# A fixed first expert, turns of half the length and a gate on the expert rows, in a two-block transformer kernel

## Chip, cores and metric

One core of a Trainium2 chip runs the whole program. The metric is the device time of one execution in microseconds (us). Weights come from the chip's memory (HBM) through one queue of DMA transfers, which the SyncE program (SP) issues. TensorE (PE) multiplies, VectorE (DVE) and ScalarE (ACT) prepare operands and empty PSUM, and GpSimd (POOL) does little.

## What is computed

256 tokens of width 1024 go through a first block (branches of attention and gated recurrence, then 32 small experts) and a second block of two layers: attention and a dense feed-forward layer, then a state-space mixer and, last, a layer of 8 large experts. The change touches only this last layer and the final norm. All is in float32. Cut to what matters:

```
def moe_swiglu(h, w_router, w_gate, w_up, w_down):      # h: 256 tokens x 1024
    top_vals, top_idx = lax.top_k(t @ w_router, 2)      # 2 of 8 experts a token
    gates = softmax over the two, spread over 8 columns
    for e in range(8):                                  # w_gate, w_up: 1024 x 2816, w_down: 2816 x 1024
        out = out + gates[:, e:e + 1] * swiglu(t, w_gate[e], w_up[e], w_down[e])
...
    x = x + g2[:, None, :] * y                          # g2: the layer gate, 1024 numbers
return rmsnorm(x, final_norm)
```

The inputs are drawn by `setup_inputs(seed=0)`. Computed from the reference with these inputs, the router sends 33, 58, 115, 44, 96, 45, 47 and 74 tokens to experts 0 to 7.

## The kernel before

**Ranks.** After the router's logits, VectorE counts the tokens of each expert and sorts the experts by count (`order_dve`, line 2096). The experts of ranks 0 to 3 are the heavy ones. Each has 128 slots for tokens, and PE multiplies it in three float32r passes per product (`split_product`, line 262), for which ACT makes the high part of each weight tile (line 192) and DVE the low part (line 202). The experts of ranks 4 to 7 are the light ones. They are computed in two pairs, numbers 4 and 5 in `RANKS`; each expert of a pair has 64 slots (`SIDE`), the two share the array by halves, and the product is in plain float32 straight from the loaded tile (lines 2458 and 2513). An expert whose tokens don't fit its slots gets a block of its own at the end (`over_cases`), with its weights loaded once more.

**Units.** An expert's weights come in units of two rows of 128 by 1024 columns, 1 MiB each. The 2816 hidden columns are three chunks, 0 to 2, of 1024, 1024 and 768 columns. A chunk of a heavy expert is 4 units of the gate matrix and 4 of the up matrix (768 KiB each in chunk 2), and the down matrix is 11 units. A pair has twice as many. The ring holds 8 units. SP issues the load of unit u as soon as unit u-8 has been let go: for a heavy expert that is when DVE has made the low parts of the unit, which it may do up to four parts (two units) ahead of PE; for a pair it is when PE has multiplied the two units of a step. One semaphore per slot holds SP.

**The order by hand.** `PHASES` says in which order experts are read in ("in": gate and up) and out ("out": down). It runs heavy 0 (in, out), pair 4 (in), heavy 1 (in, out), pair 4 (out), heavy 2 (in, out), pair 5 (in), heavy 3 (in, out), pair 5 (out). I call a stretch of work on heavy experts between two of pairs a heavy turn, and the other way round a light turn. All five engines' programs follow this list. The first load of the layer waits for the sorted order (SP line 3957), because every expert's address comes out of it.

**Around a turn.** After the gate product of a chunk PE turns the chunk before it (`mid_pe`, line 2260), and scatters the rows of an expert that has ended into token order (`scatter_pe`, through line 252), which DVE adds to `total` (line 2372). Before that the down product, which lies in PSUM, is scaled by the slots' gates and split into a high part by ACT (line 2342) and a low part by DVE (line 2407). During a light turn ACT and DVE make up to four parts of the next heavy turn ahead.

**The end.** `last_dve` multiplies `total` by the layer gate `gate_b` (line 3924), adds it to `x` (line 3925), and then comes the final norm: squares on DVE and ACT (lines 853, 840), two small operations on POOL, and the scaled output (line 3930), which SP stores.

Of the kernel before, what the change touches and what calls it, by code (L numbers as in the profile page):

```python
# [301 lines left out]
def row_parts(n, kt=KD):  # L302
# [17 lines left out]
INS = [i for phase, i in PHASES if phase == "in"]  # L320
OUTS = [i for phase, i in PHASES if phase == "out"]

# [6 lines left out]
def heavy_after(phase, i):  # L329

    n = PHASES.index((phase, i)) + 1
    return next((k for ph, k in PHASES[n:] if ph == "in" and k < HEAVY), None)

# [35 lines left out]
def block(nc, A, out):  # L369
# [180 lines left out]
    def moe_tensors(M, rows_, where):  # L550
# [11 lines left out]
        if M.three:  # L562
# [3 lines left out]
            M.key, M.top, M.order = sb("key" + t, [P, n], where=where), sb("top" + t, [P, n], where=where), sb("order" + t, [P, n], U32, where=where)  # L566
            M.order_f, M.chosen = sb("order_f" + t, [P, n], where=where), sb("chosen" + t, [P, n, n], where=where)
# [112 lines left out]
    moe2.gain8, moe2.acc = None, total  # L680
# [126 lines left out]
    for phase, i in PHASES:  # L807
        sides = range(len(RANKS[i]))
        if phase == "in":
            for ch in range(len(moe2.chunks)):  # L810
                for g in range(2):
                    for k0 in range(0, KD, moe2.kper):
                        for side in sides:
                            ranked_in_unit(i, side, g, ch, k0)
# [4 lines left out]
        units_after[phase, i] = len(fine.units)  # L819
# [1215 lines left out]
    def gates_pool(g, M):  # L2035
        g.iota(M.iota[:, :], pattern=[[1, M.n_exp]], base=0, channel_multiplier=0,
               allow_small_or_imprecise_dtypes=True).then_inc(*consts.up())
        g.iota(M.slots[:, :], pattern=[[1, P]], base=0, channel_multiplier=0,
               allow_small_or_imprecise_dtypes=True).then_inc(*consts.up())
        g.iota(M.beyond[:, :, :], pattern=[[-SIDE if M.three else P, M.blocks], [1, P]], base=M.cap, channel_multiplier=0,  # L2040
               allow_small_or_imprecise_dtypes=True).then_inc(*consts.up("iota", M.name))
# [76 lines left out]
    def ranked_table_dve(v, st, M):  # L2118
# [4 lines left out]
        v.tensor_scalar(M.over[:, 0:HEAVY], top[:, 0:HEAVY], 8.0 * P, None, ALU.is_gt).then_inc(*d.up())  # L2123
# [191 lines left out]
    def expert_act(a, run, i):  # L2315
# [16 lines left out]
        a.wait_ge(*run.multiplied(last_down(run, i)))  # L2332
        if M.three:
            y_hi_act(a, run, i)
        else:
            a.copy(M.ysb[:, :], run.banks.of(st.name, "down", i)).then_inc(*st.act.up("y", i))
# [27 lines left out]
    def scatter_dve(v, run, i):  # L2364
        M, st = run.moe, run.st
        for t in range(NT):
# [3 lines left out]
            elif run is run2:  # L2370
                v.wait_ge(*st.pool.of("total"))
# [3 lines left out]
    def expert_dve(v, run, i, e, slots):  # L2375
# [14 lines left out]
        if M.three:  # L2390
            slot_gates_dve(v, run, i)
            y_lo_dve(v, run, i)
# [10 lines left out]

    def y_lo_dve(v, run, i):
# [4 lines left out]
        run.banks.empty(st.dve, st.name, "down", i)  # L2409

    IN_CHUNKS = [(i, ch) for i in INS for ch in range(len(moe2.chunks))]

    def chunk_before(i, ch):
        n = IN_CHUNKS.index((i, ch))
        return IN_CHUNKS[n - 1] if n else None

    def turned_in(i, ch):

        b = chunk_before(i, ch)
        return b if b and (ch or b[0] >= HEAVY) else None

    def phase_before(phase, i):
        n = PHASES.index((phase, i))
        return PHASES[n - 1] if n else (None, None)
# [36 lines left out]
    def in_pe(p, i):  # L2463
        st = S["moe2"]
        held = phase_before("in", i)
        for ch, n in enumerate(moe2.chunks):
            cuts = [slice(c, min(c + 512, n)) for c in range(0, n, 512)]
            for g in range(2):
                ps = banks.take(p, "moe2", ("gate", "up")[g], i, ch)
                if ch == 0 and g == 0:  # L2470
                    if i == 0:
                        constant_products(p, ps, ident, 16)
                    if held[0] == "out" and held[1] >= HEAVY:
                        banks.let_go("moe2", "down", held[1])
                (heavy_in_product_pe if i < HEAVY else light_in_product_pe)(p, i, g, ch, ps, cuts)
                if g == 0:
                    if ch == 0 and held[0] == "out":
                        scatter_pe(p, run2, held[1])
                    if turned_in(i, ch):
                        mid_pe(p, run2, *turned_in(i, ch))  # L2480
                if i == 0 and ch == 1:
                    light_step_pe(p, g)
# [42 lines left out]
    def ranked_pe(p):  # L2525
        for step in range(4):
            pair_step_pe(p, 0, step)
        for phase, i in PHASES:
            (in_pe if phase == "in" else out_pe)(p, i)
# [4 lines left out]
    def hi_after(a, i, u):  # L2534
        fine_split.make_hi(a, min(fine_split.end(u) + PARTS, fine_split.end(out_unit(i))))

    def lo_after(v, i, u):
        fine_split.make_lo(v, min(fine_split.end(u) + PARTS, fine_split.end(out_unit(i))))

    def parts_ahead(phase, i, n):  # L2540

        k = heavy_after(phase, i)
        return fine_split.first[run2.units[k, 0, 0, 0, 0]] + n if k is not None else 0
# [21 lines left out]
    def in_act(a, i):  # L2565
        M, st = moe2, S["moe2"]
        for ch, n in enumerate(M.chunks):
            if i < HEAVY:
                hi_after(a, i, in_unit(i, 0, ch))
            a.wait_ge(*run2.multiplied(in_unit(i, 0, ch)))  # L2570
            if chunk_before(i, ch):
                a.wait_ge(*st.dve.of("mid", *chunk_before(i, ch)))
            a.activation(M.sil_row[:, 0:n], banks.of("moe2", "gate", i, ch)[:, 0:n], ACT.Silu).then_inc(*st.act.up("sil", i, ch))  # L2573
            banks.empty(st.act, "moe2", "gate", i, ch)
            if turned_in(i, ch):
                turned_mid_act(a, *turned_in(i, ch))
            if i == 0 and ch == 1:
                light_step_act(a, 0)
            if i < HEAVY:
                hi_after(a, i, in_unit(i, 1, ch))  # L2580
            if i == 0 and ch == 1:
                light_step_act(a, 1)
        if i >= HEAVY:
# [1469 lines left out]
```

## Time and profile before

| what | value |
|---|---|
| three runs | 2307.22, 2312.49, 2314.65 us, median 2312.49 |
| the profiled execution | 2311.4 us; its span of instructions is 2309.5 us |
| busy share of the span | PE 85%, PEld 61%, DVE 47%, ACT 37%, POOL 2% |
| HBM read | 659.90 MB, 286 GB/s over the span |
| first load of the last layer issued | 1575.86 us |
| last down product multiplied | about 2289.2 us |

The span is the time from the first instruction to the last; the runs' times lie around it. Rows of the profile give times in us from the start of the span.

### The profile page before, as it was taken

What the parts mean: (1) busy time and instruction counts of PE and PEld (TensorE: products, weight loads), DVE (VectorE), ACT (ScalarE), POOL (GpSimd) and SP (SyncE); (2) the same over time, 40 slices, a digit from 0 to 9 for tenths busy, and PEclk for the clock granted to TensorE, in tenths of its full rate; (3) what the DMA queues carried; (4) which work ended last, traced back from release to release, by engine and by line L of the source; (5) the groups of instructions that cost most, each with busy time, mean ns of one, the idle gap of its engine ahead of it and who ended that gap; (6) DMA issues with size and microseconds to landing.
All of it is one profiled execution on the core that took longest, in us unless ns stands there. A gap on an engine that the chain in (4) does not pass through costs nothing.

```text
span 2309.5 us, 29186 instructions
## 1 busy us (share of the span) xinstructions
PE 1952.6 (85%) x12033; PEld 1401.9 (61%) x12033; DVE 1085.1 (47%) x1661; ACT 854.1 (37%) x1153; POOL 44.9 (2%) x110
## 2 busy tenths in 40 slices
PE   6989988996656556698999998998987999997996
PEld 6968767762111111357899797877843775843772
DVE  3945556431211110233555577767830873930772
ACT  4432344310000000234444357846710754720760
POOL 0010200000000000000000000000000000000000
PEclk9989998999898888899999999999999999999998
DMA  8463662489999999859445454407999999999996
GB/s 269 168 219 110 210 244 74 189 315 393 409 409 409 409 409 409 302 198 369 147 165 201 164 155 160 143 1 286 367 383 405 406 372 409 391 379 405 407 379 244
DMA packets 227523, 663.02 MB, mean 287 GB/s; under 512 B 20100, under 2 KB 28840, under 8 KB 227124
## 3 DMA queue, kind: packets, MB, share of 16 engines
q1 hardware_dynamic: 219628, 652.92, 74.0%
q10 hardware_dynamic: 7752, 8.11, 1.3%
q8 instruction: 99, 1.62, 0.3%
q14 instruction: 44, 0.36, 0.1%
HBM read 659.90 MB, written 1.10 MB: 286 GB/s over the span
## 4 chain that ended last, share of the span: by engine, by line
PE 52%; DMA 25%; DVE 12%; ACT 7%; issue 3%; POOL 0%; ACTq 0%; SPq 0%; DVEq 0%; POOLq 0%
PE psum L263 11%; PE psum L265 11%; PE psum L264 11%; PE psum L252 6%; DMA ring<-in_w_expert_down 6%; DMA ring<-in_w_expert_up 5%; DMA ring<-in_w_expert_gate 5%; DMA ring<-in_moe_w_gate 4%; PE psum L2458 3%; DMA ring<-in_moe_w_up 3%; PE psum L2513 2%; DVE w_lo L202 2%; PE psum L2738 2%; ACT w_hi L192 2%; PE psum L1175 1%
## 5 line engine op out<-in xcount | busy, mean ns | idle before, releaser
L202 DVE TENSOR_TENSOR w_lo<-ring,w_hi 128x1024 fp32r<-128x1024 f32 (+1 forms) x498 | 579.4, 1187 | 389.4 <-ACT w_hi L192 380.6
L192 ACT CAST w_hi<-ring 128x1024 fp32r<-128x1024 f32 (+1 forms) x498 | 502.9, 1021 | 335.8 <-PE psum L265 297.0
L2738 PE MATMUL psum<-ring,hT 128*32 128x512 f32 x960 | 145.5, 738 | 117.1 <-DMA ring<-in_w_expert_gate 63.8
L2458 PE MATMUL psum<-ring,xg_pair 128*64 128x512 f32 (+1 forms) x768 | 159.8, 561 | 38.8 <-DMA ring<-in_moe_w_gate 19.9
L2738 PEld LDWEIGHTS psum<-ring,hT 128*32 128x32 f32 x960 | 30.3, 124 | 228.0 <-issue 97.5
L263 PE MATMUL psum<-w_hi,xg_hi 128*128 128x512 f32 (+1 forms) x384 | 146.4, 381 | 7.3 <-DVE w_lo L202 7.3
L264 PE MATMUL psum<-w_hi,xg_lo 128*128 128x512 f32 (+1 forms) x384 | 145.1, 378 | 0.0
L265 PE MATMUL psum<-w_lo,xg_hi 128*128 128x512 f32 (+1 forms) x384 | 144.8, 377 | 0.0
L2458 PEld LDWEIGHTS psum<-ring,xg_pair 128*64 128x64 f32 x768 | 58.9, 137 | 136.7 <-issue 134.8
L2372 DVE TENSOR_TENSOR x<-x,psum 128x1024 f32<-128x1024 f32 x14 | 17.1, 1221 | 219.8 <-PE psum L252 219.8
L2760 PE MATMUL psum<-ring,midT 128*32 128x512 f32 x480 | 69.9, 712 | 44.0 <-DMA ring<-in_w_expert_down 43.5
L263 PE MATMUL psum<-h_f_hi,w_hi 128*128 128x256 f32 x352 | 100.6, 286 | 2.2 <-DVE h_f_lo L886 2.2
L264 PE MATMUL psum<-h_f_hi,w_lo 128*128 128x256 f32 x352 | 100.3, 285 | 0.0
L265 PE MATMUL psum<-h_f_lo,w_hi 128*128 128x256 f32 x352 | 100.2, 285 | 0.0
L263 PEld LDWEIGHTS psum<-w_hi,xg_hi 128*128 128x128 f32 x384 | 72.6, 189 | 24.4 <-issue 7.7
L2513 PE MATMUL psum<-ring,midT 128*64 128x512 f32 x352 | 78.4, 596 | 7.1 <-DMA ring<-in_moe_w_down 7.1
L265 PEld LDWEIGHTS psum<-w_lo,xg_hi 128*128 128x128 f32 x384 | 72.7, 189 | 14.3
L264 PEld LDWEIGHTS psum<-w_hi,xg_lo 128*128 128x128 f32 x384 | 72.7, 189 | 13.9
L2573 ACT ACTIVATE hT<-psum 128x1024 f32<-128x1024 f32 (+1 forms) x18 | 17.1, 951 | 166.8 <-PE psum L2458 166.8
L263 PE MATMUL psum<-w_hi,midT_hi 128*128 128x512 f32 x176 | 70.1, 398 | 3.0 <-DVE w_lo L202 3.0
L263 PE MATMUL psum<-h_mix_hi,w_hi 128*128 128x256 f32 x224 | 63.8, 285 | 7.8 <-DVE w_lo L202 7.8
L2760 PEld LDWEIGHTS psum<-ring,midT 128*32 128x32 f32 x480 | 14.2, 121 | 91.9 <-DMA ring<-in_w_expert_down 65.4
(697 smaller groups left out, 3799.0 us busy)
## 6 DMA issues: line engine op xcount, KB each, us to landing
ring<-in_moe_w_down SPq DMA_DIRECT2D x88, 1024.0 KB, 7.9
ring<-in_w_expert_gate SPq DMA_DIRECT2D x32, 2048.0 KB, 17.2
ring<-in_moe_w_gate SPq DMA_DIRECT2D x64, 1024.0 KB, 13.2
ring<-in_moe_w_up SPq DMA_DIRECT2D x64, 1024.0 KB, 14.5
ring<-in_w_expert_down SPq DMA_DIRECT2D x30, 2048.0 KB, 18.1
ring<-in_w_expert_up SPq DMA_DIRECT2D x28, 2048.0 KB, 17.9
ring<-in_ada_w SPq DMA_DIRECT2D x24, 2048.0 KB, 11.7
ring<-in_moe_w_gate SPq DMA_DIRECT2D x32, 768.0 KB, 12.1
```

The lines of the kernel that those rows point to most:

```text
L192: a.copy(self.buffers(n, src.shape)[0], src).then_inc(*self.hi_made.up())
L202: v.tensor_tensor(lo, src, hi.bitcast(F32), SUB).then_inc(*self.lo_made.up())
L252: ins = p.matmul(o, l, r, start=n == 0, stop=n == len(terms) - 1)
L263: p.matmul(o, l[0], r[0], start=start, stop=False)
L264: p.matmul(o, l[1], r[0], start=False, stop=False)
L265: return p.matmul(o, l[0], r[1], start=False, stop=stop)
L1175: ins = p.matmul(ps[32 * quarter:32 * quarter + 32, 0:256], cond[:, k:k + 1].to_broadcast([P, 32]), w[quarter // 2][:, k, c0:c0 + 256], st ...
L2372: v.tensor_tensor(M.acc[:, t, :], M.acc[:, t, :], run.banks.of(st.name, "scatter", i, t), ADD).then_inc(*st.dve.up("acc", i, t))
L2458: ins = p.matmul(ps[r, cut], moe2.xg_pair[:, i - HEAVY, k0 + k, r], w[side][:, k, cut], start=k0 + k == 0, stop=k0 + k == KD - 1)
L2513: ins = p.matmul(ps[r, cut], M.midT[:, k0 + k, r], w[side][:, k, cut], start=first, stop=last)
L2738: ins = p.matmul(ps[slots_of(j), g * 512:(g + 1) * 512], M.xg[:, 2 * q + k, slots_of(j)], w[:, j, k, :], start=2 * q + k == 0, stop=2 * q ...
L2760: ins = p.matmul(ps[slots_of(j), cut], M.midT[:, q, slots_of(j)], w[:, j, cut], start=q == 0, stop=q == 3)
```

## The change

It has three parts. First, expert 0 always takes rank 0: its key gets 4096 added, so that it comes first in the sort whatever its count, and SP loads its first eight units with a known address while the ring's last slots of the mixer become free, before the router has run. Second, the list is by chunk instead of by phase: a heavy turn is now two chunks, or the third chunk and the down product, and between them lies one chunk of a pair or its down product. Third, the layer gate is multiplied onto the expert's rows before they are split (`y_gated_dve`), the scattered rows are added straight into `x`, and `total`, its clearing on POOL and the two operations at the end go away. Besides, 12 small products on a constant stand before the last scatter, and the light experts' rows are gathered earlier (after chunk 0 and in chunk 1 of heavy 0).

```
+FIXED = 0
+FIRST_KEY = 4096.0
-PHASES = (("in", 0), ("out", 0), ("in", 4), ("in", 1), ("out", 1), ("out", 4),
-          ("in", 2), ("out", 2), ("in", 5), ("in", 3), ("out", 3), ("out", 5))
+OUT = 3
+STEPS = ((0, 0), (0, 1), (4, 0), (0, 2), (0, OUT), (4, 1), (1, 0), (1, 1), (4, 2), (1, 2), (1, OUT), (4, OUT),
+         (2, 0), (2, 1), (5, 0), (2, 2), (2, OUT), (5, 1), (3, 0), (3, 1), (5, 2), (3, 2), (3, OUT), (5, OUT))
...
-    moe2.gain8, moe2.acc = None, total
+    moe2.gain8, moe2.acc = None, x
+    y_gated = total[:, 0, :]
...
+            g.memset(M.less[:, FIXED:FIXED + 1], -FIRST_KEY).then_inc(*consts.up())
+            g.iota(M.less[:, FIXED + 1:], pattern=[[1, M.n_exp - FIXED - 1]], base=FIXED + 1, channel_multiplier=0,
...
-        settle(v, v.scalar_tensor_tensor(M.key[:, :], counts, 8.0, M.iota[:, :], MUL, SUB), d)
+        settle(v, v.scalar_tensor_tensor(M.key[:, :], counts, 8.0, M.less[:, :], MUL, SUB), d)
...
     def y_hi_act(a, run, i):
-        a.wait_ge(*st.dve.of("selgT", i))
-        a.activation(M.y_split[0], run.banks.of(st.name, "down", i), ACT.Copy, scale=M.slot_gate[:, 0:1]).then_inc(*st.act.up("y", i))
+        a.wait_ge(*st.dve.of("y_gated", i))
+        a.copy(M.y_split[0], y_gated).then_inc(*st.act.up("y", i))
...
+    def y_gated_dve(v, run, i, multiplied):
+        v.wait_ge(*multiplied)
+        v.wait_ge(*gates_loaded.of("layer", 1))
+        v.wait_ge(*st.dve.of("selgT", i))
+        v.scalar_tensor_tensor(y_gated, run.banks.of(st.name, "down", i), M.slot_gate[:, 0:1], gate_b[:, 1, :], MUL, MUL)...
...
     def y_lo_dve(v, run, i):
-        v.scalar_tensor_tensor(M.y_split[1], run.banks.of(st.name, "down", i), M.slot_gate[:, 0:1], M.y_split[0].bitcast(F32),
-                               MUL, SUB).then_inc(*st.dve.up("y_lo", i))
+        v.tensor_tensor(M.y_split[1], y_gated, M.y_split[0].bitcast(F32), SUB).then_inc(*st.dve.up("y_lo", i))
...
     def ranked_pe(p):
-        for phase, i in PHASES:
-            (in_pe if phase == "in" else out_pe)(p, i)
+        for i, ch in STEPS:
+            if ch == OUT:
+                out_pe(p, i)
+            else:
+                in_pe(p, i, ch)
+        constant_products(p, banks.held_by("moe2", "selgT", OUTS[-1])[:, 512:1024], ident, 12)
...
     def in_dve(v, i, ch):
...
+        if (i, ch) == (HEAVY, 0):
+            ranked_table_dve(v, st, M)
         if i >= HEAVY:
-            fine_split.make_lo(v, parts_ahead("in", i, PARTS))
+            fine_split.make_lo(v, parts_ahead(i, ch, PARTS))
...
-        g.memset(total[:, :, :], 0.0).then_inc(*S["moe2"].pool.up("total"))
...
-        settle(v, v.tensor_tensor(total[:, :, :], total[:, :, :], gate_b[:, 1, :].unsqueeze(1).to_broadcast([P, NT, D]), MUL), d)
-        settle(v, v.tensor_tensor(x[:, :, :], x[:, :, :], total[:, :, :], ADD), d, "x")
...
     def last_act(a):
-        a.wait_ge(*st.dve.of("x"))
+        a.wait_ge(*S["moe2"].dve.of("acc", OUTS[-1], 0))
...
     def sync(s):
+        experts = {0: FIXED}
         for u in range(len(ring.units) - SLOTS, len(ring.units)):
             if ring.emptied is not None:
                 s.wait_ge(*ring.emptied[u])
-        s.wait_ge(*S["moe2"].dve.of("order"))
-        experts = {}
+            if u % SLOTS == u - len(ring.units) + SLOTS:
+                fine.load(s, 2 * (u % SLOTS) + 2, experts)
+        ordered = False
+        for i, ch in STEPS:
+            if ch == 0:
+                if i and not ordered:
+                    s.wait_ge(*S["moe2"].dve.of("order"))
```

## Rows read from the trace of the kernel before

**Rows 1.** The page, part 2: the span in 40 equal slices of 57.7 us.

```profile
GB/s 269 168 219 110 210 244 74 189 315 393 409 409 409 409 409 409 302 198 369 147 165 201 164 155 160 143 1 286 367 383 405 406 372 409 391 379 405 407 379 244
```

**Rows 2.** The windows view of all engines: stretch, length, busy, clock, DMA share, GB/s.

```profile
1575.00:1587.00 12.00, 8.96 (x64) 8.89 (x64) 4.48 (x17) 6.39 (x11) 0.00 (x0) 0.86 0.82 321
1587.00:1697.00 110.00, 109.08 (x523) 85.03 (x524) 86.74 (x80) 76.07 (x80) 0.00 (x0) 1.00 0.98 372
...
1790.00:1897.00 107.00, 104.14 (x484) 82.10 (x482) 89.22 (x86) 75.86 (x78) 0.00 (x0) 0.98 0.98 387
...
1940.00:2047.00 107.00, 104.83 (x488) 81.73 (x489) 89.47 (x83) 73.60 (x76) 0.00 (x0) 1.00 0.99 383
2047.00:2143.00 96.00, 76.39 (x376) 29.97 (x372) 4.79 (x4) 5.41 (x6) 0.00 (x0) 1.00 1.03 407
2143.00:2248.00 105.00, 102.07 (x478) 80.71 (x480) 88.88 (x86) 75.22 (x78) 0.00 (x0) 1.00 1.00 391
...
2284.00:2310.00 26.00, 7.25 (x26) 3.72 (x24) 12.03 (x9) 2.26 (x3) 0.94 (x2) 0.71 0.11 44
```

**Rows 3.** The waits view of SP's queue, 1500 to 2310 us.

```profile
SPq L3957 <- DVE order L2101: 28.0, 1, 28.0
```

**Rows 4.** The chain that ended last, in order of time: start, us, what.

```profile
1587.10 0.43 PE psum L263
...
1621.24 0.87 PE psum L2260 x8
1622.11 1.88 PE psum L252 x16
...
1687.45 13.91 PE psum L2458 x64
...
1828.79 0.87 PE psum L2260 x8
...
1849.27 0.87 PE psum L2260 x8
...
1891.27 7.02 PE psum L2513 x32
...
2039.66 13.91 PE psum L2458 x64
...
2242.28 7.02 PE psum L2513 x32
```

**Rows 5.** The timeline of PE where heavy turns begin and the last unit lands.

```profile
1792.88 0.68 PE L263 MATMUL psum<-w_hi,xg_hi 128*128 128x512 f32 x1 [2.11 <-DVE w_lo L202]
...
1939.78 0.47 PE L263 MATMUL psum<-w_hi,xg_hi 128*128 128x512 f32 x1 [1.24 <-DVE w_lo L202]
...
1942.83 0.50 PE L263 MATMUL psum<-w_hi,xg_hi 128*128 128x512 f32 x1 [1.42 <-DVE w_lo L202]
...
2144.92 0.47 PE L263 MATMUL psum<-w_hi,xg_hi 128*128 128x512 f32 x1 [2.10 <-DVE w_lo L202]
...
2285.54 3.65 PE L2513 MATMUL psum<-ring,midT 128*64 128x512 f32 x16 [1.38 <-DMA ring<-in_moe_w_down]
```

**Rows 6.** The chain again: the end.

```profile
2289.23 1.12 ACT ysb_hi L2342
2290.38 1.29 DVE ysb_lo L2407
2291.81 3.45 PE psum L252 x8
...
2296.70 2.30 DVE total L3924
2299.03 2.30 DVE x L3925
```

**Rows 7.** The timeline of DVE in the first light turn: the overflow table's first and last operation.

```profile
1720.58 0.15 DVE L2123 TENSOR_SCALAR over<-top 1x4 f32<-1x4 f32 x1
...
1725.30 0.16 DVE L2133 CAST table<-tf 1x10 int32<-1x10 f32 x1
```

More of the change, by code:

```diff
@@ L326, in out_before, with heavy_after, heavy_end @@
     return OUTS[n - 1] if n else None
-def heavy_after(phase, i):
-    n = PHASES.index((phase, i)) + 1
-    return next((k for ph, k in PHASES[n:] if ph == "in" and k < HEAVY), None)
+def heavy_after(i, ch):
+    n = STEPS.index((i, ch)) + 1
+    return next((step for step in STEPS[n:] if step[0] < HEAVY), None)
+def heavy_end(i, ch):
+    n = STEPS.index((i, ch))
+    while n + 1 < len(STEPS) and STEPS[n + 1][0] < HEAVY:
+        n += 1
+    return STEPS[n]
 class Moe:
@@ L806, in block @@
     units_after = {}
-    for phase, i in PHASES:
+    for i, ch in STEPS:
         sides = range(len(RANKS[i]))
[L809 to L814, printed above, removed]
+        if ch != OUT:
+            for g in range(2):
+                for k0 in range(0, KD, moe2.kper):
+                    for side in sides:
+                        ranked_in_unit(i, side, g, ch, k0)
         else:
@@ L818, in block @@
                     ranked_out_unit(i, side, k0)
-        units_after[phase, i] = len(fine.units)
+        units_after[i, ch] = len(fine.units)
+    assert len(ring.units) % SLOTS == 0, len(ring.units)
     split_ends = (split.end(unit["out", 1]), len(split.parts))
@@ L2391, in expert_dve @@
             slot_gates_dve(v, run, i)
+            y_gated_dve(v, run, i, run.multiplied(last_down(run, i)))
             y_lo_dve(v, run, i)
@@ L2461, in light_in_product_pe, with in_pe @@
                 fine.empty(st.pe, u)
[L2463 to L2482, printed above, removed]
+    def in_pe(p, i, ch):
+        n = moe2.chunks[ch]
+        ended = out_ended(i, ch)
+        cuts = [slice(c, min(c + 512, n)) for c in range(0, n, 512)]
+        for g in range(2):
+            ps = banks.take(p, "moe2", ("gate", "up")[g], i, ch)
+            if g == 0:
+                if (i, ch) == (0, 0):
+                    constant_products(p, ps, ident, 16)
+                if ended is not None and ended >= HEAVY:
+                    banks.let_go("moe2", "down", ended)
+            (heavy_in_product_pe if i < HEAVY else light_in_product_pe)(p, i, g, ch, ps, cuts)
+            if g == 0:
+                if ended is not None:
+                    scatter_pe(p, run2, ended)
+                if turned_in(i, ch):
+                    mid_pe(p, run2, *turned_in(i, ch))
+            if (i, ch, g) == (0, 0, 1):
+                light_step_pe(p, 0)
+            if (i, ch, g) == (0, 1, 0):
+                light_step_pe(p, 1)
     def out_pe(p, i):
@@ L2532, in ranked_pe, with step_end, hi_after, lo_after @@
         over_pe(p, run2, over2)
[L2534 to L2543, printed above, removed]
+    def step_end(i, ch):
+        return fine_split.end(out_unit(i) if ch == OUT else in_unit(i, 1, ch))
+    def hi_after(a, i, ch, u):
+        fine_split.make_hi(a, min(fine_split.end(u) + PARTS, step_end(*heavy_end(i, ch))))
+    def lo_after(v, i, ch, u):
+        fine_split.make_lo(v, min(fine_split.end(u) + PARTS, step_end(*heavy_end(i, ch))))
+    def parts_ahead(i, ch, n):
+        step = heavy_after(i, ch)
+        if step is None:
+            return 0
+        k, c = step
+        return fine_split.first[run2.units[(k, 0, 2, 0) if c == OUT else (k, 0, 0, c, 0)]] + n
     def turned_mid_act(a, i, ch):
@@ L2563, in mid_lo_dve, with in_act @@
         banks.empty(st.dve, "moe2", "mid", i, ch)
-    def in_act(a, i):
+    def in_act(a, i, ch):
         M, st = moe2, S["moe2"]
[L2567 to L2583, printed above, removed]
-            fine_split.make_hi(a, parts_ahead("in", i, PARTS))
+        n = M.chunks[ch]
+        if i < HEAVY:
+            hi_after(a, i, ch, in_unit(i, 0, ch))
+        a.wait_ge(*run2.multiplied(in_unit(i, 0, ch)))
+        if chunk_before(i, ch):
+            a.wait_ge(*st.dve.of("mid", *chunk_before(i, ch)))
+        a.activation(M.sil_row[:, 0:n], banks.of("moe2", "gate", i, ch)[:, 0:n], ACT.Silu).then_inc(*st.act.up("sil", i, ch))
+        banks.empty(st.act, "moe2", "gate", i, ch)
+        if turned_in(i, ch):
+            turned_mid_act(a, *turned_in(i, ch))
+        if (i, ch) == (0, 1):
+            light_step_act(a, 1)
+        if i < HEAVY:
+            hi_after(a, i, ch, in_unit(i, 1, ch))
+        else:
+            fine_split.make_hi(a, parts_ahead(i, ch, PARTS))
+        if (i, ch) == (0, 0):
+            light_step_act(a, 0)
     def out_act(a, i):
@@ new lines, in in_dve @@
+                ranked_selg_dve(v, i)
+            lo_after(v, i, ch, in_unit(i, 0, ch))
+        if ended is not None:
+            scatter_dve(v, run2, ended)
+        if (i, ch) == (0, 0):
+            light_select_dve(v)
+        if turned and turned[0] < HEAVY:
+            mid_lo_dve(v, *turned)
+        if i < HEAVY:
+            lo_after(v, i, ch, in_unit(i, 1, ch))
+        else:
+            fine_split.make_lo(v, parts_ahead(i, ch, 1))
+        v.wait_ge(*st.act.of("sil", i, ch))
+        v.wait_ge(*run2.multiplied(in_unit(i, 1, ch)))
```

108 lines of the change are left out of this document (51 added, 57 removed).

## The prediction

> **What bounds the kernel now.** I read the page's slices first. In [rows 1] the last layer, from slice 28 on, moves 367 to 409 GB/s, and slice 27 before it moves 1 GB/s. So the layer is close to the rate of the DMA engines, and ahead of it lies a hole. Then I cut the layer by turns [rows 2]. A light turn runs at 407 GB/s while PE works 76 of 96 us: it waits for weights. The four heavy turns run at 372, 387, 383 and 391 GB/s with PE busy nearly throughout: there PE is the slower one, the ring fills, and SP finds no free slot. Last I read the chain for the instant at which each turn begins [rows 4, 5] and for the end [rows 6].
>
> Full rate is 410 GB/s (the rate of undisturbed stretches, which the light turn is within 1% of), so a unit of 1 MiB takes 1.0486/0.410 = 2.56 us. The layer has 264 MiB: 675.2 us. [Rows 2] give what the queue idles: 110 x 38/410 = 10.2 us in the turn of heavy 0, then 6.0, 7.0 and 4.9 us in the other three (each with the switch to the pair behind it), and 3/410 of some 270 us of light turns, 2.0 us; in all 30.1. In 1575 to 1587 the queue moved 321 x 12 = 3.85 MB, 9.4 us of work, so data flow from 1577.6. The sum, 1577.6 + 675.2 + 30.1 = 2282.9, is 2.6 us short of the last unit's landing at 2285.5 [rows 5], which I carry along as the way from the last byte to PE. The layer's time is thus its bytes plus 30 us of idle queue. Behind the landing lie 2309.5 - 2285.5 = 24.0 us.
>
> **The change: the head start.** SP's wait for the order lasted 28.0 us [rows 3] and ended with the sort at about 1574.7, so the mixer's last slot was free at 1546.7. Eight units need 20.5 us and fit into that hole. They don't move PE's first product: before it come the gather of rows and constant products, which end at 1587.1 [rows 4]. From there PE takes 34.1 us for three half chunks (to 1621.24), 0.9 for turning, 1.9 for each of two gather steps, which now both lie here, and 11.2 for the fourth half chunk: 1637.1. The 11.2 is from the next turn: from 1828.79 to 1849.27 are 20.5 us, less 0.9 for turning, for a half chunk of 1024 and one of 768 columns, 11.2 + 8.4. The first step of the pair takes 13.91/4 = 3.5 us: at 1640.6 it lets two slots go. The ring was full from 1587 on, so by then exactly 16 units of heavy 0 and 8 of the pair are in; and that would be so without the head start too, since 24 units need 61.4 us and 1577.6 + 61.4 = 1639.0 is before 1640.6. My sum therefore gives the head start nothing: what it loads early is idled away in front of a full ring.
>
> **The change: the order.** Data flow again about 2.2 us after a slot is let go (I estimate this from the 9.4 us above: 1.8 from the issue at 1575.86 to the data, and 0.4 for the issue), at 1642.8. 240 MiB remain: 613.8 us, plus 2.0 for the rate of light turns. With no further idle the last unit lands at 1642.8 + 613.8 + 2.0 + 2.6 = 2261.2, 24.3 us sooner than now.
>
> How much idle is left? In the old turns PE took 98.4, 99.9 and 97.4 us ([rows 5] to [rows 4]: 1792.88 to 1891.27, 1939.78 to 2039.66, 2144.92 to 2242.28) for 84.4 us of transfers. It fell 14.0, 15.5 and 13.0 us behind, and 6.0, 7.0 and 4.9 us were idled. Each time about 8.2 us of lag cost nothing. That is the room of the ring as seen from a turn's start. In front of chunk 2 of a pair eight units of 768 KiB hold 15.3 us instead of 20.5 and the first step is 0.9 us shorter, so the room is 4.0.
>
> The new turns: two chunks are 44.8 us of products, two turnings of 0.9 and 0.3 of waiting, 46.9, against 40.9 of transfers: lag 6.0. Chunk 2 and down are 16.9 + 22 parts of 1.4 us (11.2/8) + 0.9 + 0.7 + 1.2 (gates' turning and waiting) = 50.5 against 43.5: lag 7.0. A light turn waits for weights by 9 us or more (chunk: 28.7 against 40.9; chunk 2: 21.8 against 30.7) and clears either. So most turns cost nothing. Four do. Behind chunk 0 of pair 4 DVE now builds the overflow table, 4.9 us [rows 7], between the first and the second part of the next heavy turn; a part in hand covers 1.4, so 7.0 + 3.5 - 8.2 = 2.3. Heavy 1 and heavy 3 go from two chunks into chunk 2 of a pair: 6.0 - 4.0 = 2.0 each. Heavy 2 starts behind a pair's down product, with the scatter (1.0 more than a turning), the 1.4 us wait for DVE at 1942.83 and 1.3 for the new operation: 9.7 - 8.2 = 1.5. Together 7.8, and 0.7 for a slow clock (below): 8.5. Landing at 2269.7, 15.8 us sooner.
>
> The clock: after the wait at 1792.88 [rows 5] the first products take 0.68 us instead of 0.47, the lower level of 1.2 GHz, and the turn's stretch has a granted clock of 0.98; after the other two waits, 1939.78 and 2144.92, it stayed at full speed. One switch in three loses about 1.7 us (107 x 0.02 = 2.1 at most). Seven switches into heavy turns instead of three put some 2.3 us more lag on PE, of which I let 0.7 reach the queue. The Trainium skill speaks against the change here: "TensorE: Matmul & The Clock Gate", section "HAM oscillation", says that a wait for a transfer between bursts of products throws the clock back each time. By it all seven would start slow; the trace has one in three.
>
> **The gate on rows.** Six times 1.3 us of DVE are added, the kind of the 1.29 at 2290.38. Behind a heavy expert they lie beside the pair's gate product (13.9 us), and nothing waits; uncovered all six would be 7.7 us. POOL's clearing was beside other work. At the end the two operations at 2296.70 and 2299.03 go: 4.6 us. The chain from the down product to the scatter gets one DVE operation more: +1.2 (ACT and DVE then read the gated rows instead of PSUM at about the same cost). The clock of that stretch is 0.71 [rows 2], and 8 products take 3.45 us; the 12 constant products fill the wait, so the scatter may run in 1.9. As DVE's addition of the first half (1.2) then ends it, I count 1.1 of the 1.6. At the end: -4.6 - 1.1 + 1.2 = -4.5.
>
> **Sum.** -15.8 - 4.5 = -20.3 us on the profiled execution (2311.4 us, span 2309.5), which lies 1.1 us under the median of 2312.49. 2312.5 - 20.3 = 2292.2; I say 2292.
>
> **The rivals.**
> *Larger gain, the head start counts (12%).* Had the ring not filled at the start, the 8 units less the 3.7 that were in by 1587 would be worth 11.0 us: 2281. For it speaks only the hole; against it that heavy 0 idled 10.2 us already [rows 2]. No later idle at all, at full clock, gives 2283.5.
> *Only the end gains (10%).* The idle queue stays at the old sum, seven switches of 3.5 us each: the turns are shorter but as many us are lost to full slots. -4.5 us: 2308, within the noise.
> *Slower through switches (7%).* Each new switch costs the queue what an old one does, 6.0 us on average. Seven are 42 us, 33.5 more than in my sum: 2325.5. It decides from 4.1 us a switch (8.5 + 20.3 = 28.8 over seven). For it: the idle lies partly at the switch itself, where a slot waits for a pair's first step. Against: the lags of 6 and 7 us are under the room that three turns agree on.
> *An expert overflows (3%).* Expert 0 takes a heavy rank whatever its count, and a fifth busy expert falls among the light ones with 64 slots. With the counts of the default inputs the light ones are 58, 47, 45, 44: none overflows. Were it so, one expert more is 84.4 us of weights: above 2376.
> *As forecast (68%).* 2282 to 2304.
>
> **Range and chances.** Low end 2280: no later idle, or the head start. High end 2304: later idle as now (17.9 instead of 8.5) and no warmer clock at the end, 2292.2 + 9.4 + 1.1 = 2302.7, rounded up for the spread of the runs. About 0.3%, 7 us, is what a measurement can tell. Faster: 68 + 12 = 80%. Same 10%. Slower 7 + 3 = 10%.
>
> **What would show it.** In the profile after: 8 units landed before 1557; PE's first product still near 1587; hardly any transfer idle after 1643, but 10 to 15 us of idle between 1587 and 1643, where the head start goes; the pair's first step near 1637; four stretches of idle of some 2 us near the ends of heavy turns; last landing near 2270, and 19.5 us behind it. I'm wrong if heavy turns' stretches stay under 395 GB/s (the room is smaller than 8.2), if PE starts sooner than 1585, if PE's clock is 0.9 in most heavy turns, or if an expert's weights are loaded a second time.

## The result, and the profile after

The kernel after took 2297.39 us (median of four runs, 2294.58 to 2299.20) beside 2312.25 for the kernel before on the same chip: the ratio is 0.9936, with a 95% interval of 0.9923 to 0.9950. That is 14.9 us less. Forecast were 20.3 us less, 2292. The profiled execution took 2299.2 us and has a span of 2297.4.

I read the same views as before. First the page's slices, which answer to [rows 1]:

```profile
GB/s 262 177 220 109 186 241 73 218 282 393 409 409 409 409 409 409 325 177 369 169 184 184 199 132 145 177 121 154 331 394 386 390 408 409 387 407 409 388 408 276
```

The hole of 1 GB/s in slice 27 is now 121 GB/s: most of the eight units are loaded in it. But slice 28 has gone from 286 down to 154 and slice 29 from 367 to 331: the queue waits, because the ring is full sooner. Then SP's issues in the timeline (start, us until the last of the group, what):

```profile
1500.73 19.79 SPq L139 DMA_DIRECT2D ring<-in_moe_w_gate  x4
1536.50 13.78 SPq L139 DMA_DIRECT2D ring<-in_moe_w_up  x4
1590.77 2.64 SPq L139 DMA_DIRECT2D ring<-in_moe_w_gate  x2
```

The eight units are asked for by 1550.3 us; from there SP issues nothing until PE works. Next the windows view, with the columns of [rows 2]; the first stretch is the start, the others are the eight heavy turns, each with its switch to the pair behind it:

```profile
1500.00:1557.00 57.00, 53.22 (x248) 43.04 (x247) 36.63 (x48) 27.07 (x40) 3.56 (x4) 0.95 0.43 153
1590.00:1643.00 53.00, 52.83 (x248) 41.49 (x249) 40.94 (x36) 36.42 (x38) 0.00 (x0) 1.00 0.85 317
1690.00:1743.00 53.00, 52.22 (x246) 36.35 (x247) 34.77 (x33) 28.44 (x29) 0.00 (x0) 1.00 0.96 370
1770.00:1820.00 50.00, 50.00 (x244) 36.68 (x243) 33.94 (x29) 28.61 (x29) 0.00 (x0) 1.00 1.00 390
1840.00:1890.00 50.00, 49.21 (x240) 38.50 (x240) 41.44 (x43) 33.32 (x36) 0.00 (x0) 1.00 1.03 408
1938.00:2000.00 62.00, 59.06 (x255) 42.38 (x256) 44.95 (x40) 34.87 (x34) 0.00 (x0) 0.97 0.99 388
2022.00:2076.00 54.00, 52.74 (x260) 41.72 (x262) 44.08 (x43) 35.79 (x38) 0.00 (x0) 1.00 1.03 408
2108.00:2160.00 52.00, 51.46 (x240) 39.49 (x240) 41.12 (x37) 34.37 (x34) 0.00 (x0) 1.00 1.00 391
2183.00:2236.00 53.00, 52.22 (x256) 41.37 (x258) 44.17 (x45) 35.75 (x38) 0.00 (x0) 1.00 1.03 408
```

The second row is the first heavy turn, with the ring full: 53 x (410 - 317)/410 = 12.0 us of idle queue. Of the other heavy turns three run at 408 GB/s and four, the third, fourth, sixth and eighth row, lose 5.2, 2.4, 3.3 and 2.4 us. Last the chain that ended last, which answers to [rows 4] and [rows 6]:

```profile
1589.79 0.43 PE psum L263
...
1639.64 13.88 PE psum L2485 x64
...
2278.05 3.67 PE psum L2541 x16
2281.74 1.29 DVE total L2427
2283.06 1.05 ACT ysb_hi L2360
2284.14 1.24 DVE ysb_lo L2433
2285.42 1.21 PE psum L252 x4
2286.65 1.23 DVE x L2388
2287.93 1.09 DVE x L2388
2289.21 1.24 DVE total L866 x2
...
2293.02 1.20 DVEq L4076
```

For the comparisons below I cut each profile at two points, PE's first product of heavy 0 (1587.06 us before, 1589.75 after; it moves by some us from one execution to the next, with work that the change doesn't touch) and the start of the last unit's product (2285.54 before [rows 5], 2278.05 after). Between them lies the **layer**, behind them the **end**. **Late idle** is the queue's idle time from 70 us after the first point on, summed over stretches of 10 us, each counted as (410 - its GB/s)/41; a last stretch in which the last bytes land is left out. Before: layer 698.5, end 24.0, late idle 24.6, and 4.8 in the first 70 us. After: layer 688.3, end 19.4, late idle 16.0, and 14.1 in the first 70 us. So 10.2 us came from the layer and 4.6 from the end.

### The profile page after: what moved, and what is told of

It reads as the page before. It is cut to its first block, busy times and chain, and to the rows that moved or that the text cites. A ratio compares the mean times of both kernels' runs of the same rounds, so it can differ in the third digit from the quotient of the medians.

```text
span 2297.4 us, 29176 instructions
## 1 busy us (share of the span) xinstructions
PE 1958.5 (85%) x12057; PEld 1405.4 (61%) x12057; DVE 1088.2 (47%) x1666; ACT 852.3 (37%) x1153; POOL 43.3 (2%) x111
## 3 DMA queue, kind: packets, MB, share of 16 engines
HBM read 659.90 MB, written 1.10 MB: 288 GB/s over the span
## 4 chain that ended last, share of the span: by engine, by line
PE 53%; DMA 23%; DVE 13%; ACT 7%; issue 3%; POOL 0%; ACTq 0%; SPq 0%; DVEq 0%; POOLq 0%
PE psum L263 11%; PE psum L265 11%; PE psum L264 11%; PE psum L252 6%; DMA ring<-in_w_expert_down 6%; DMA ring<-in_w_expert_up 5%; DMA ring<-in_w_expert_gate 5%; PE psum L2485 4%; DMA ring<-in_moe_w_gate 3%; DVE w_lo L202 3%; PE psum L2782 2%; ACT w_hi L192 2%; DMA ring<-in_moe_w_down 2%; PE psum L2541 2%; PE psum L1188 1%
## 5 line engine op out<-in xcount | busy, mean ns | idle before, releaser
L2388 DVE TENSOR_TENSOR x<-x,psum 128x1024 f32<-128x1024 f32 x26 | 31.2, 1219 | 251.8 <-PE psum L252 251.8
L259 PE MATMUL psum<-ident 128*128 128x128 f32 x582 | 72.4, 283 | 0.0
L259 PEld LDWEIGHTS psum<-ident 128*128 128x128 f32 x582 | 70.1, 199 | 2.1 <-issue 1.6
L2804 PEld LDWEIGHTS psum<-ring,midT 128*32 128x32 f32 x480 | 14.5, 122 | 92.4 <-DMA ring<-in_w_expert_down 65.0
## 6 DMA issues: line engine op xcount, KB each, us to landing
ring<-in_moe_w_gate SPq DMA_DIRECT2D x32, 768.0 KB, 11.2
```

What stands on the lines that cost most here:

```text
L259: p.matmul(o[:, 0:P], constant[:, :], constant[:, :], start=True, stop=True)
L2388: v.tensor_tensor(M.acc[:, t, :], M.acc[:, t, :], run.banks.of(st.name, "scatter", i, t), ADD).then_inc(*st.dve.up("acc", i, t))
L2804: ins = p.matmul(ps[slots_of(j), cut], M.midT[:, q, slots_of(j)], w[:, j, cut], start=q == 0, stop=q == 3)
```

## The experiments

Each is the kernel after with one edit, except "table earlier, two parts", which has two, and the last two. The ratio is to the kernel before, run on the same chip as the version; the versions were spread over three chips, so compare ratios, not medians. A ratio is uncertain by 2 to 5 us, while the layer of a profile is steadier: the four profiles after, PE held in light turns, no constant products and after again give 688.0 to 688.3.

| run | median us | ratio to before | layer | end | late idle |
|---|---|---|---|---|---|
| before | 2312.25 | 1 | 698.5 | 24.0 | 24.6 |
| after | 2297.39 | 0.9936 (0.9923 to 0.9950) | 688.3 | 19.4 | 16.0 |
| no head start | 2297.04 | 0.9942 (0.9925 to 0.9959) | 689.7 | 19.3 | 17.3 |
| long turns | 2308.24 | 0.9986 (0.9975 to 0.9997) | 701.1 | 19.4 | 27.1 |
| table earlier | 2292.30 | 0.9919 (0.9899 to 0.9940) | 683.7 | 19.3 | 11.3 |
| gate at the end | 2297.82 | 0.9945 (0.9924 to 0.9966) | 686.5 | 23.8 | 14.5 |
| table earlier, two parts | 2290.04 | 0.9907 (0.9888 to 0.9925) | 681.4 | 19.3 | 8.2 |
| PE held in light turns | 2297.39 | 0.9940 (0.9920 to 0.9959) | 688.3 | 19.4 | 16.1 |
| PE held in heavy turns | 2308.24 | 0.9983 (0.9971 to 0.9994) | 699.5 | 19.3 | 27.1 |
| no constant products | 2296.70 | 0.9936 (0.9919 to 0.9952) | 688.0 | 20.8 | 16.1 |
| head start alone | 2310.74 | 0.9999 (0.9989 to 1.0009) | 695.9 | 23.9 | 21.9 |
| after again | 2295.86 | 0.9935 (0.9921 to 0.9949) | 688.2 | 19.4 | 15.8 |

**No head start.** SP waits for the order in front of the first load, so nothing of the layer is loaded early.

```
-            if u % SLOTS == u - len(ring.units) + SLOTS:
-                fine.load(s, 2 * (u % SLOTS) + 2, experts)
-        ordered = False
+        s.wait_ge(*S["moe2"].dve.of("order"))
...
```

> The changed kernel, but SP waits for the sorted order before its first load, as before; all else stays. Theory A (the ring is full again before the pair's first step, so the head start is idled away): same as the changed kernel, 14.9 us under the kernel before (2297.4), and the transfer queue idles some 11 us less between PE's first product and the first light turn. Rival (the head start is the gain, 8 units less the 3.7 that came anyway, 11.0 us): about 2308, 4 us under the kernel before.

The layer took 1.4 us longer and the median is the same within its interval; that the 1.4 us are the head start's is not shown. The windows view of this run shows why, against the second row of the fence above:

```profile
1574.00:1590.00 16.00, 16.00 (x94) 14.60 (x95) 8.51 (x10) 12.20 (x16) 0.00 (x0) 0.89 1.03 413
1590.00:1643.00 53.00, 52.84 (x251) 38.31 (x252) 34.39 (x30) 31.01 (x32) 0.00 (x0) 1.00 0.96 376
```

The eight units are now loaded from 1574 us on at full rate, and the queue idles 53 x 34/410 = 4.4 us in the first turn instead of 12.0. Over the whole first 70 us of the layer it is 4.4 instead of 14.1: 9.7 us less, where some 11 were expected.

**Long turns.** The order of before, with all else as after. A light chunk prepares parts of a heavy turn only if this turn is the next step.

```
...
+STEPS = ((0, 0), (0, 1), (0, 2), (0, OUT), (4, 0), (4, 1), (4, 2), (1, 0), (1, 1), (1, 2), (1, OUT), (4, OUT),
+         (2, 0), (2, 1), (2, 2), (2, OUT), (5, 0), (5, 1), (5, 2), (3, 0), (3, 1), (3, 2), (3, OUT), (5, OUT))
...
-        if step is None:
+        if step is None or STEPS[STEPS.index((i, ch)) + 1] != step:
```

> The changed kernel with the old order of work: whole heavy experts between the pairs' in and out turns; head start, gate on rows and the end stay new. Theory A (the shorter turns bring all of the gain within the layer, 10.2 us by the trace): 4.6 us under the kernel before, 2307.7, and four stretches of idle queue as before. Rival (the head start brings it): 14.9 us or more under it, 2297.

The layer is 12.8 us longer and late idle 11.1 us more; the end is the same. This profiled execution took 2310.98 us, 2.7 more than the run's median, so the layer of a typical one is shorter; by the ratios the two kernels are 11.6 us apart. The turns' length is where nearly all of the layer's gain comes from.

**Table earlier.** The overflow table was built by DVE between the first and the second part of heavy 0's chunk 2. Here it is built before the first part, while PE multiplies pair 4's chunk 0.

```
         if turned and turned[0] < HEAVY:
             mid_lo_dve(v, *turned)
+        if (i, ch) == (HEAVY, 0):
+            ranked_table_dve(v, st, M)
...
-        if (i, ch) == (HEAVY, 0):
-            ranked_table_dve(v, st, M)
         if i >= HEAVY:
             fine_split.make_lo(v, parts_ahead(i, ch, PARTS))
```

> The changed kernel with the overflow table built while PE multiplies the first light turn, instead of between the first and second part of the heavy turn behind it. Theory A (the 5.8 us in which PE waits for DVE there fill the ring, and the turn idles the queue 5.2 us in place of the 2.3 forecast; without the table a lag of 7.0 is under the room of 8.2): 5 us under the changed kernel, 2292.4. Rival (the queue is idle there for another reason, the ring still full from the start): no change, 2297.4.

The layer fell by 4.6 us and late idle by 4.7, as expected; the table now starts 67 us behind PE's first product instead of 83. First the timelines of PE and DVE in the kernel after (start, us, engine, line, operation; in brackets the idle time before it and what ended it):

```profile
1671.50 0.47 PE L263 MATMUL psum<-w_hi,xg_hi 128*128 128x512 f32 x1 [0.16 <-DVE w_lo L202]
...
1678.57 0.79 PE L263 MATMUL psum<-w_hi,xg_hi 128*128 128x512 f32 x1 [5.78 <-DVE w_lo L202]
1679.16 0.63 PE L264 MATMUL psum<-w_hi,xg_lo 128*128 128x512 f32 x1
```

```profile
1671.43 1.22 DVE L2683 TENSOR_TENSOR ada_row<-hT,psum 128x1024 f32<-128x1024 f32 x1
1672.57 0.13 DVE L2140 TENSOR_SCALAR over<-top 1x1 f32<-1x1 f32 x1
...
1677.36 0.16 DVE L2151 CAST table<-tf 1x10 int32<-1x10 f32 x1
1677.56 3.56 DVE L202 TENSOR_TENSOR w_lo<-ring,w_hi 128x768 fp32r<-128x768 f32 x4
```

And PE in the run with the table earlier:

```profile
1669.09 0.48 PE L263 MATMUL psum<-w_hi,xg_hi 128*128 128x512 f32 x1 [0.22 <-DVE w_lo L202]
...
1671.11 0.50 PE L263 MATMUL psum<-w_hi,xg_hi 128*128 128x512 f32 x1 [0.72 <-DVE w_lo L202]
```

In the kernel after PE waited 5.78 us for the second part, and its products then took 0.63 instead of 0.40 us, the lower clock level. With the table earlier the wait is 0.72 us, and the clock stayed.

**Gate at the end.** The two operations of before stand at the end again, with `total`, its clearing, and the split read from PSUM; the one operation on the rows goes.

```
...
-        a.copy(M.y_split[0], y_gated).then_inc(*st.act.up("y", i))
...
+        a.activation(M.y_split[0], run.banks.of(st.name, "down", i), ACT.Copy, scale=M.slot_gate[:, 0:1]).then_inc(*st.act.up("y", i))
...
-            y_gated_dve(v, run, i, run.multiplied(last_down(run, i)))
...
+        settle(v, v.tensor_tensor(total[:, :, :], total[:, :, :], gate_b[:, 1, :].unsqueeze(1).to_broadcast([P, NT, D]), MUL), d)
+        settle(v, v.tensor_tensor(x[:, :, :], x[:, :, :], total[:, :, :], ADD), d, "x")
```

> The changed kernel with the layer gate at the end again: rows split straight out of PSUM, total cleared by POOL and added to x at the end; order, head start and the 12 constant products stay new. Theory A (the gate on rows is worth the 4.6 us of the two operations less 1.2 for one more DVE operation in the last chain, and hidden elsewhere): 3.5 us over the changed kernel, 2300.9. Rival (the six added DVE operations delay heavy turns, so that taking them away gives something back): 1 to 2 us over it.

The end is 4.4 us longer, the layer 1.8 us shorter: 2.6 us in the profiles, where 3.5 were expected, and 2 by the ratios, which are too coarse to tell that from nothing. So the theory holds for the end, and the rival has a part in the layer. The place of the 1.8 is where heavy 2 starts behind the down product of pair 4. PE's timeline and the windows view here, then the same of the kernel after:

```profile
1937.45 0.50 PE L263 MATMUL psum<-w_hi,xg_hi 128*128 128x512 f32 x1 [1.42 <-DVE w_lo L202]
...
1937.45:1947.45 10.00, 10.00 (x43) 8.09 (x44) 9.78 (x11) 6.97 (x7) 0.00 (x0) 1.00 1.03 411
```

```profile
1942.09 0.50 PE L263 MATMUL psum<-w_hi,xg_hi 128*128 128x512 f32 x1 [2.94 <-DVE w_lo L202]
...
1942.09:1952.09 10.00, 10.00 (x36) 8.01 (x37) 8.76 (x10) 5.64 (x6) 0.00 (x0) 0.83 1.02 407
```

The operation on the rows makes PE wait 2.94 us instead of 1.42, and behind the longer wait the clock fell: 0.83 granted over the next 10 us, some 1.7 us of PE's time. Together 3.2 us more lag for PE, and 2.8 us of idle queue in the stretch at 400 us of the layer, where this run has under 0.5.

**Table earlier, two parts.** The same edit as in "table earlier" (not shown again), and DVE makes two parts of the next heavy turn, not one, before it turns to the light chunk's own rows.

```
-fine_split.make_lo(v, parts_ahead(i, ch, 1))
+fine_split.make_lo(v, parts_ahead(i, ch, 2))
...
-fine_split.make_lo(v, parts_ahead(i, OUT, 1))
+fine_split.make_lo(v, parts_ahead(i, OUT, 2))
```

> The kernel with the early table (18.6 us under the kernel before), and DVE now makes two low parts of the next heavy turn ahead of a pair's last operations instead of one. Theory A (heavy 2 starts behind a pair's down product with a wait of 2.9 us for DVE and products at half clock behind it; its turn idles the queue 3.2 us, and with the wait gone its lag falls under the room): 3 us less again, 2289. Rival (the scatter and the gate on rows make that turn long, not the wait): no change, 2292.

This is the fastest version: 2290.04 us, and 6.9 us less in the layer than after, 2.3 less than with the early table alone. Late idle fell to 8.2 us. But the theory's reason did not come: the longer wait behind pair 4 was left (2.78 us) and only stands behind the second part now, not the first. In this profile the clock stayed at full speed after it, and idle there fell from 2.8 to 1.3 us. Whether making two parts keeps the clock up, or this one execution had luck, is not shown.

**PE held in light turns.** PE does 12 steps of products on a constant (24 instructions) before the up product of each chunk of a pair.

```
+            if g == 1 and i >= HEAVY:
+                constant_products(p, ps, ident, 12)
```

> The changed kernel with 12 constant products (2.8 us of PE) before the up product of each chunk of a pair, six times, 16.8 us in all. Theory A (in a light turn PE waits 9 to 12 us for weights, so its own work is free there): the changed kernel's time, 2297.4, within 2 us. Rival (PE's work is what counts in the whole layer): up to 16.8 us more, 2314.

Six times 2.84 us, 17 us of PE in all, cost nothing: the layer took the same 688.3 us, and the ratio is 0.9940 beside 0.9936. In a light turn PE waits for weights, as the forecast had it.

**PE held in heavy turns.** The same before the up product of the first chunk in each of the seven heavy turns that follow a light one.

```
+            if g == 1 and i < HEAVY and (i, ch) != (0, 0) and step_before(i, ch)[0] >= HEAVY:
+                constant_products(p, ps, ident, 12)
```

> The changed kernel with the same 12 constant products before the up product of the first chunk of each heavy turn behind a light one, seven times, 19.6 us in all. Theory A (a lag over the room of 8.2 us, or 4.0 before a pair's chunk 2, is lost): four turns are over already and lose 2.8 each, three have 1.2 left and lose 1.6 each: 16.0 us more, 2313.4. Rivals: nothing, since the transfers bound the layer as a whole, 2297.4; or all 19.6.

Now 19.6 us of PE (seven times 2.8) cost 11.2 us of layer. That is between the two rivals, and less than the 16.0 us of the theory. The windows view gives the place. First the kernel after, from 70, 160, 240, 300, 430, 500 and 590 us behind its first product:

```profile
1659.75:1749.75 90.00, 80.81 (x378) 53.13 (x376) 53.43 (x75) 40.12 (x43) 0.00 (x0) 0.96 0.99 385
1749.75:1829.75 80.00, 76.36 (x374) 49.65 (x370) 44.13 (x39) 38.50 (x38) 0.00 (x0) 1.00 1.01 396
1829.75:1889.75 60.00, 56.70 (x282) 43.73 (x282) 47.01 (x49) 38.32 (x42) 0.00 (x0) 1.00 1.03 407
1889.75:2019.75 130.00, 120.05 (x544) 66.40 (x540) 52.52 (x53) 44.51 (x48) 0.00 (x0) 0.99 1.01 399
2019.75:2089.75 70.00, 68.18 (x330) 47.97 (x328) 48.60 (x47) 38.63 (x42) 0.00 (x0) 1.00 1.03 408
2089.75:2179.75 90.00, 81.66 (x400) 51.84 (x396) 44.15 (x39) 38.92 (x39) 0.00 (x0) 1.00 1.01 396
2179.75:2259.75 80.00, 75.56 (x366) 50.51 (x364) 50.37 (x53) 38.47 (x42) 0.00 (x0) 1.00 1.03 408
```

And this run, the same distances from its own:

```profile
1655.86:1745.86 90.00, 80.91 (x388) 55.02 (x386) 53.26 (x75) 40.29 (x43) 0.00 (x0) 0.96 0.97 372
1745.86:1825.86 80.00, 77.29 (x384) 51.23 (x382) 44.59 (x40) 38.72 (x38) 0.00 (x0) 1.00 0.99 386
1825.86:1885.86 60.00, 55.62 (x296) 43.82 (x293) 42.90 (x42) 38.02 (x41) 0.00 (x0) 1.00 1.03 407
1885.86:2015.86 130.00, 124.36 (x570) 71.93 (x570) 56.64 (x57) 44.19 (x47) 0.00 (x0) 0.97 0.99 387
2015.86:2085.86 70.00, 65.89 (x332) 48.32 (x330) 46.89 (x45) 39.19 (x42) 0.00 (x0) 1.00 1.02 404
2085.86:2175.86 90.00, 87.52 (x428) 55.21 (x426) 45.91 (x41) 39.55 (x39) 0.00 (x0) 1.00 0.99 390
2175.86:2255.86 80.00, 76.50 (x392) 53.53 (x390) 51.24 (x54) 39.07 (x42) 0.00 (x0) 1.00 1.03 407
```

The first, second, fourth and sixth row, which hold the turns that were idle already, lose 2.9, 2.0, 3.8 and 1.3 us more (such as 90 x 13/410), together 9.9 of the 11.2 us that PE is held in them. The other three, with the turns of chunk 2 and down of heavy 1, 2 and 3, lose 0.9 us together. So turns that are over the room of the ring pass on most of what they are made to lag, though unevenly, and a turn of chunk 2 and down still has nearly 2.8 us to spare. The theory's miss is in these three: it had 4.8 us for them.

**No constant products.** The 12 steps of constant products before the last scatter are left out.

```
-        constant_products(p, banks.held_by("moe2", "selgT", OUTS[-1])[:, 512:1024], ident, 12)
```

> The changed kernel without the 12 constant products before the last scatter. Theory A (they keep the clock up; the scatter of a row half takes 1.2 us instead of 2.1 and the second one follows sooner): 1.1 us more, 2298.5, and L252 at about 0.43 us a product. Rival (without the clock nothing is lost, since DVE's additions set the pace): no change.

The end took 1.4 us longer in the profile, where 1.1 were expected; the medians are too coarse to show it. PE's timeline at the last scatter:

```profile
2281.61 0.80 PE L252 MATMUL psum<-ysb_hi,selgT 128*128 128x512 f32 x1 [3.71 <-DVE ysb_lo L2433]
2282.20 0.63 PE L252 MATMUL psum<-ysb_lo,selgT 128*128 128x512 f32 x1
```

Its products take 0.63 us; in the kernel after they take 0.40.

**Head start alone, and after again.** The last pair ran on one chip with one kernel before. Head start alone has the order of before (as in "long turns") and the gate of before (as in "gate at the end"); of the change it keeps the fixed expert 0, the early loads of its first eight units, the earlier gather of the light experts' rows and the constant products. (The expectation below speaks of two units in the light turns; the kernel that ran has expert 0 as the first heavy one, as in the change.) After again is the kernel after, unchanged.

> The kernel before's order of steps and its layer gate at the end, with expert 0 first in the light turns, its two units asked for ahead of the sorting, and twelve constant products kept. The theory that the head start is worth next to nothing: the layer takes 698 to 701 us and the end 23.8 us, so the median is within 0.3% of the kernel before, near 2312. The rival that the whole unused time of the queue during the sorting comes off the time: about 11 us less, near 2301.

> The kernel after itself, unchanged, beside the run above on the same chip: its median 0.993 to 0.995 of the kernel before's, so that the difference between the two runs is what turns half as long and the gate on rows give together, expected at 14 to 15 us. The rival, that the head start carries a good part of it, wants 5 us or less between the two.

Head start alone took 0.9999 of before's time (0.9989 to 1.0009, so at most 2.5 us less), and the kernel after 0.9935 again. The rival with 11 us is out by a wide margin. In its profile the layer is 2.6 us shorter than before; 1.7 of them may be the clock, which stayed at full speed through this layer and fell behind the wait at 1792.88 in the one before (0.83 over 10 us). By the ratios of three steps, head start alone 0.9999, with the gate on rows 0.9986 (long turns), with short turns 0.9935 or 0.9936, the three parts are worth some 0, 3 and 12 us. Each ratio is uncertain by 2.3 to 3.2 us and so each difference of two by 3 to 4: the 12 us are clear, the 3 us are not.

## Why the prediction was right, and where a size was off

**What bounds the layer: right.** (The forecast skips a slice in its first reading: behind the slice with 1 GB/s comes one with 286 and then those with 367 to 409 GB/s. No term of the sum rests on it.) The layer's time is its bytes plus the idle of the queue in every version here: between after and "table earlier" both fell by 4.6 to 4.7 us, between after and "long turns" they rose by 12.8 and 11.1 (and the idle of the first 70 us by 1.5), and 17 us of work for PE in the light turns added nothing.

**The head start gives nothing: right.** PE's first product was forecast near 1587 and came at 1589.75, 2.7 us later, a difference that this profile has already in its first 130 us, where the two kernels are the same. From there the forecast to the pair's first product was 50.0 us (1637.1 less 1587.1), and 49.9 were measured. The idle of 10 to 15 us between 1587 and 1643 is there, 12.0. The forecast asked for 8 units landed before 1557: 153 GB/s x 57 us are 8.7 MB, and eight units are 8.4 MB.

**The order: the mechanism right, the gain 5.6 us smaller.** The layer was forecast to fall by 15.8 us and fell by 10.2. The term of the sum that was too small is the idle that is left: 8.5 us in four turns and 2.0 us of lower rate, against 16.0 measured. By place (idle of the stretches of 10 us around each switch):

| place | forecast | measured |
|---|---|---|
| table, in chunk 2 and down of heavy 0 | 2.3 | 4.7 |
| heavy 1 into chunk 2 of pair 4 | 2.0 | 2.1 |
| heavy 2, behind pair 4's down | 1.5 | 2.8 |
| heavy 3 into chunk 2 of pair 5 | 2.0 | 2.5 |
| slow clock, spread over the turns | 0.7 | in the rows above |
| everywhere else | 2.0 | 3.9 |

*The table* is the largest miss. I let "a part in hand" cover 1.4 us of DVE's 4.9 and had a wait of 3.5 us. But a part of chunk 2 is smaller, PE needs 1.1 us for it, and DVE's operation on the light chunk's own rows, 1.2 us, comes in between as well: the cover was used up before the table began, and PE waited 5.78 us, of which 0.72 remain without the table. So the table cost a wait of 5.1 us where the forecast had 3.5. The half clock behind it, 0.77 granted over 10 us, is 2.3 us more. The moved table gives the 4.7 us back, which shows this cause.

*Heavy 2* starts late because the new operation on the rows lengthens PE's wait, as forecast (1.4 and 1.3, against 2.94 measured), but I had not tied the clock to it. The sum counted the slow start as a share of 0.7 us over all turns; it fell on a turn that was over the room already, where it is paid in full.

*The room of the ring* was well sized for turns of two chunks: 4.0 us before a pair's chunk 2 (2.0 of idle forecast, 2.1 and 2.5 measured), and 8.2 before pair 5's chunk 0 (a lag of 9.7 and 1.7 for the clock, less 8.2, is 3.2; measured 2.8). For turns of chunk 2 and down, 8.2 was too small: with a lag of 7.0 us and 2.8 more they cost nearly nothing, so there it is at least 9.8 us. The table's turn says the same: 7.0 + 5.1 + 2.3 of lag less 4.7 of idle is 9.7. This error went the other way and hid part of the table's, which is luck: with a room of 8.2 that turn would have idled the queue by 6.2 us instead of 4.7. The forecast's own sign for a smaller room, heavy turns under 395 GB/s, came true in four of seven (370, 390, 388 and 391) without the room being smaller; the sign was too strict, since 2.4 us of idle in 50 are 390 GB/s already. The 1.9 us in "everywhere else" I have not traced.

**The clock: nearly right in number.** Of the seven switches into a heavy turn two started at the lower level, in the profile of after again three, where one in three, 2.3, was forecast. All twelve profiles together, for PE's waits for DVE and by the clock granted over the 10 us from the end of a wait: after the 32 waits of 1.0 to 1.4 us that had no longer one close behind it was 1.00 each time; after nine waits of 2.1 to 2.3 us it was 0.83 five times; after nine of 2.8 to 3.0 us (all at heavy 2, with one of 1.24 us just ahead) it was 0.69 to 0.83 eight times; after seven of 5.8 us always 0.73 to 0.79. Waits for weights behave much alike: of seven of 2.1 to 2.7 us three were followed by 0.83, in no constant products, the fastest version and after again, all just ahead of heavy 1's chunk 2, and the others by 1.00. So the clock's loss went with the length of PE's wait, not with the number of switches. The Trainium skill, "TensorE: Matmul & The Clock Gate", section "HAM oscillation", describes a loop whose waits of some 3 to 5 us for transfers throw the clock back each time. The forecast read more into it when it let all seven switches start slow by it: six of the seven waits are under 3 us here. For the waits of 5.8 us the trace agrees, seven of seven. That shorter waits than those of that loop can do it too, 13 of the 18 of 2.1 to 3.0 us, is what the rows here show, and those up to 1.4 us show no loss.

**The gate on rows: right at the end, missed in the layer.** From the last unit's product to the last row of the chain were 19.6 us before, 2285.54 to this row:

```profile
2305.16 1.20 DVEq L4031
```

With the constant products alone it is 18.5 (head start alone, gate at the end), so they gave 1.1, as forecast. With the gate on rows it is 15.0: 3.5 us less, where 4.6 less 1.2 were forecast. The whole end is 4.6 us shorter against 4.5. In the two runs with constant products and the gate at the end, what lies behind this last row took 5.3 and 5.4 us, against 4.3 before and 4.4 after, so that their whole end is hardly shorter than before's; why is open. But what I costed at nothing in the layer, beyond the 1.3 in heavy 2's lag, cost 1.8 us, by the rows of the two runs mainly through the clock. What the whole part is worth is not settled: 0.0009 of the time between after and gate at the end and 0.0013 between head start alone and long turns are 2 and 3 us, neither clear of the intervals; the profiles of the first pair give 2.6, and in those of the second the layer took 5.2 us more for 4.5 less at the end.

**The rivals.** "The head start counts" (2281) is refuted by the run with it alone. "Only the end gains" (2308) is what "long turns" measured, 2308.24, and the kernel after is some 11 to 12 us under it. "Slower through switches" (2325.5) needed 6.0 us a switch, and 4.1 to be slower at all; seven switches lost 12.1 us together, 1.7 each. "An expert overflows" did not come: no second load of an expert is in the page, and HBM read is 659.90 MB in both.

## What to carry to other kernels

Where a fixed number of slots sits between a queue and an engine, cost a change of order turn by turn: lag of the engine less the room of the ring, at next to nothing if negative and at most of its size if positive (here 0.9 of 8.4 us and 9.9 of 11.2). Measure the room for each kind of turn: the 8.2 us, taken from turns of a whole expert, were at least 9.8 for turns of chunk 2 and down. A load moved into a hole gained nothing here, because the ring was full again before the next stretch ended; look at how long the queue idles there before counting the hole. And small serial work on a helper engine belongs where it has a whole light product as cover: the table of 4.9 us cost 4.7 us in one place, and 16 us earlier on the same engine none that the layer shows.

## What the runs showed of the hardware

A wait of the same length leads to half speed once and not another time: in the kernel before, 2.11 us at 1792.88 were followed by a granted clock of 0.83 over 10 us, and 2.10 us at 2144.92, in front of the same kind of turn, by 1.00. A wait that is 1.5 us longer (2.94 instead of 1.42 behind pair 4) cost up to 3.2 us of TensorE's time. And TensorE's work in stretches where it waits for weights was free here: 17 us of extra products left the layer at 688.3 us.
